# Transfers of 16x16 diagonal blocks through memory, issued by GpSimd in place of ScalarE

## The reference

```python
L = jnp.where(strict, jnp.einsum('nbhcd,nbhsd->nbhcs', k_beta, kb) * decay, 0.0)
eye = jnp.eye(C, dtype=L.dtype)
tinv = lax.linalg.triangular_solve(eye + L, jnp.broadcast_to(eye, L.shape),
                                   left_side=True, lower=True, unit_diagonal=True)
u = jnp.einsum('nbhcs,nbhse->nbhce', tinv, v_beta)
w = jnp.einsum('nbhcs,nbhsd->nbhcd', tinv, k_beta * jnp.exp(gc)[..., None])
```

## Time and profile before

| | us |
|---|---|
| median of 3 runs | 2109.6 (2106.55 to 2113.05) |
| the profiled execution, its own time | 2120.13 |
| its span | 2118.4 |
| TensorE busy | 1952.8 (92%) |
| DVE busy | 1248.9 (59%) |
| ACT busy | 939.3 (44%) |
| GpSimd busy | 4.9 (0%) |

### The profile page before, as it was taken

One profiled execution on the slowest core, in us unless ns is written; L12 is line 12 of the kernel. 1 busy time (PEld: TensorE's weight loads), 2 busy tenths in 40 slices (PEclk: granted clock), 3 DMA queues, 4 the chain that ended last, 5 costly groups with the idle time before them and its releaser, 6 DMA issues.

```text
span 2118.4 us, 45367 instructions
## 1 busy us (share of the span) xinstructions
PE 1952.8 (92%) x19408; PEld 1762.3 (83%) x19408; DVE 1248.9 (59%) x2135; ACT 939.3 (44%) x1834; POOL 4.9 (0%) x30
## 2 busy tenths in 40 slices
PE   6999989899999997899999999988899989879998
PEld 4899968788878876788989998878898778669898
DVE  3455356665445575677556655566654565758863
ACT  3334464344456434333444444544445653343343
POOL 0000000000000000000000000000000000000000
PEclk8999999999999898899999999999899998889999
DMA  7777765556464456698656665544534345267773
GB/s 257 229 228 212 213 172 151 159 145 169 120 177 127 130 150 159 178 265 238 191 158 185 182 176 165 162 123 125 140 103 139 100 117 140 82 138 223 231 199 113
DMA packets 580070, 353.37 MB, mean 167 GB/s; under 512 B 44004, under 2 KB 539654, under 8 KB 578318
## 3 DMA queue, kind: packets, MB, share of 16 engines
q1 hardware_dynamic: 490634, 302.74, 49.7%
q10 hardware_dynamic: 89236, 47.74, 9.1%
HBM read 332.27 MB, written 18.50 MB: 166 GB/s over the span
## 4 chain that ended last, share of the span: by engine, by line
PE 72%; DVE 11%; DMA 7%; ACT 5%; issue 3%; ACTq 3%; SPq 0%; DVEq 0%
PE bank L881 69%; DMA ring<-in_ffn_up 2%; DVE far L1931 2%; DVE ring_r L733 2%; DMA ring<-in_w_ada 2%; ACT w_hi_r L725 1%; DMA far<-in_state_gdn_ssm 1%; DVE big L1931 1%; PE bank L659 1%; ACTq L572 1%; DVE far L1934 1%; PE bank L646 1%; DMA far<-t_blocks 1%; ACTq L627 1%; DVE big L608 1%
## 5 line engine op out<-in xcount | busy, mean ns | idle before, releaser
L881 PE MATMUL bank<-big_r,w_hi_r 128*128 128x264 f32 x4160 | 1082.5, 295 | 37.5 <-DVE h_r L1934 22.7
L881 PE MATMUL bank<-big_r,ring_r 128*128 128x264 f32 (+1 forms) x3456 | 1001.1, 290 | 0.0
L881 PEld LDWEIGHTS bank<-big_r,w_hi_r 128*128 128x128 f32 x4160 | 756.1, 193 | 105.1 <-issue 78.7
L881 PE MATMUL bank<-h_r,w_hi_r 128*128 128x264 f32 x2752 | 804.1, 292 | 0.0
L733 DVE TENSOR_TENSOR ring_r<-ring,w_hi_r 128x1024 fp32r<-128x1024 f32 (+2 forms) x440 | 524.5, 1195 | 466.2 <-ACT w_hi_r L725 462.1
L725 ACT CAST w_hi_r<-ring 128x1024 fp32r<-128x1024 f32 (+2 forms) x440 | 452.3, 1028 | 498.2 <-PE bank L881 262.3
L881 PEld LDWEIGHTS bank<-big_r,ring_r 128*128 128x128 f32 (+1 forms) x3456 | 669.9, 194 | 1.0
L881 PEld LDWEIGHTS bank<-h_r,w_hi_r 128*128 128x128 f32 x2752 | 537.7, 195 | 1.2
L881 PE MATMUL bank<-big,far 64*64 64x64 f32 (+2 forms) x1440 | 106.6, 260 | 0.0
L881 PE MATMUL bank<-ring,c 128*32 128x256 f32 x1152 | 95.4, 413 | 9.4 <-DMA ring<-in_w_ada 6.4
L1931 DVE TENSOR_TENSOR big<-big,bank 128x264 f32<-128x264 f32 (+2 forms) x138 | 62.8, 458 | 56.1 <-PE bank L881 44.2
(11 more groups left out here) (283 smaller groups left out, 1843.7 us busy)
## 6 DMA issues: line engine op xcount, KB each, us to landing
ring<-in_ffn_up SPq DMA_DIRECT2D x176, 512.0 KB, 4.6
ring<-in_w_in SPq DMA_DIRECT2D x148, 512.0 KB, 3.7
ring<-in_w_ada SPq DMA_DIRECT2D x144, 512.0 KB, 4.0
ring<-in_ffn_down SPq DMA_DIRECT2D x64, 512.0 KB, 4.3
far<-in_state_gdn_ssm ACTq DMA_DIRECT2D x28, 512.0 KB, 5.7
ring<-in_ffn_down SPq DMA_DIRECT2D x32, 384.0 KB, 3.5
ring<-in_w_out SPq DMA_DIRECT2D x16, 512.0 KB, 4.7
out_sample_gdn_ssm<-far ACTq DMA_DIRECT2D x16, 512.0 KB, 4.1
```

What stands on the lines that cost most here:

```text
L881: return pe.matmul(out, lhsT, rhs, start=start, stop=stop)
```

## The change

The transfers of the diagonal blocks are issued by GpSimd. Its program for a layer is these 54 transfers and nothing else, in a fixed order, lot by lot, with the waits that ACT had. ACT's program keeps the clearing. The first lot's substitution stands in turns 24 and 25 of DVE's program in place of 20 and 21; the other two lots keep their turns.

```diff
-GATHER0, FETCH0, SOLVE0, STORE0 = (18, 30, 66), (19, 31, 67), (20, 32, 68), (22, 34, 69)
-CLEAR0, SCATTER0, INV0 = (29, 35, 67), (30, 36, 70), (32, 38, 72)
+SOLVE0, CLEAR0, INV0 = (24, 32, 68), (29, 35, 67), (32, 38, 72)
...
-        def gather(act, run):
+        def gather(pool, run):
             lt = inv_sets[run][0]
             if run == 2:
-                act.wait_ge(gdn_dve.sem, gdn_dve.at(H_B - 1))
+                pool.wait_ge(gdn_dve.sem, gdn_dve.at(H_B - 1))
             else:
-                act.wait_ge(prod_dve.sem, prod_dve.at(4 * run + 4))
+                pool.wait_ge(prod_dve.sem, prod_dve.at(4 * run + 4))
...
             for rows, cols, part_of in blocks():
-                act.dma_start(lt_blocks[part_of, :, :].rearrange("u s t -> s u t"), lt[rows, :, cols]).then_inc(block_in.sem, block_in.one())
+                pool.dma_start(lt_blocks[part_of, :, :].rearrange("u s t -> s u t"), lt[rows, :, cols]).then_inc(block_in.sem, block_in.one())
...
             for l in range(DEPTH):
+
+                @block.gpsimd
+                def _(pool):
+                    for run in range(3):
+                        gather(pool, run)
+                        fetch(pool, run)
+                        store(pool, run)
+                        scatter(pool, run)
...
                         for run in range(3):
-                            if t == GATHER0[run] and run < 2:
-                                gather(act, run)
-                            if t == FETCH0[run]:
-                                fetch(act, run)
-                            if t == STORE0[run] and run < 2:
-                                store(act, run)
-                            if t == SCATTER0[run]:
-                                scatter(act, run)
                             if t - INV0[run] == 3:
                                 settled(act, run)
...
-                        if t == GATHER0[2]:
-                            gather(act, 2)
-                        if t == STORE0[2]:
-                            store(act, 2)
...
-                        if t == STORE0[1] + 3:
+                        if t == SOLVE0[1] + 5:
```

More of the change, by code:

```diff
@@ L560, in square, with fetch, store @@
             return buf.rearrange("p (a b) -> p a b", a=B16)
-        def gather(act, run):
+        def gather(pool, run):
             lt = inv_sets[run][0]
             if run == 2:
-                act.wait_ge(gdn_dve.sem, gdn_dve.at(H_B - 1))
+                pool.wait_ge(gdn_dve.sem, gdn_dve.at(H_B - 1))
             else:
-                act.wait_ge(prod_dve.sem, prod_dve.at(4 * run + 4))
+                pool.wait_ge(prod_dve.sem, prod_dve.at(4 * run + 4))
             if run:
-                act.wait_ge(block_in.sem, block_in.at(9 * run))
+                pool.wait_ge(block_in.sem, block_in.at(9 * run))
             for rows, cols, part_of in blocks():
-                act.dma_start(lt_blocks[part_of, :, :].rearrange("u s t -> s u t"), lt[rows, :, cols]).then_inc(block_in.sem, block_in.one())
-        def fetch(act, run):
-            act.wait_ge(block_in.sem, block_in.at(9 * run + 8))
+                pool.dma_start(lt_blocks[part_of, :, :].rearrange("u s t -> s u t"), lt[rows, :, cols]).then_inc(block_in.sem, block_in.one())
+        def fetch(pool, run):
+            pool.wait_ge(block_in.sem, block_in.at(9 * run + 8))
             if run:
[L578 to L583, removed]
+                pool.wait_ge(solved.sem, solved.at(run))
+            pool.dma_start(square(solve_bufs[run][0]), lt_blocks[:, :, :]).then_inc(block_in.sem, block_in.one())
+        def store(pool, run):
+            pool.wait_ge(solved.sem, solved.at(run + 1))
             if run:
-                act.wait_ge(block_out.sem, block_out.at(9 * run))
-            act.dma_start(t_blocks[:, :, :, :], solve_bufs[run][1]).then_inc(block_out.sem, block_out.one())
+                pool.wait_ge(block_out.sem, block_out.at(9 * run))
+            pool.dma_start(t_blocks[:, :, :, :], solve_bufs[run][1]).then_inc(block_out.sem, block_out.one())
         def solve(dve, run, half):
@@ L619, in clear, with scatter @@
             i.then_inc(inv_z.sem, inv_z.one())
-        def scatter(act, run):
-            act.wait_ge(inv_z.sem, inv_z.at(run + 1))
-            act.wait_ge(block_out.sem, block_out.at(9 * run + 1))
+        def scatter(pool, run):
+            pool.wait_ge(inv_z.sem, inv_z.at(run + 1))
+            pool.wait_ge(block_out.sem, block_out.at(9 * run + 1))
             into = inv_sets[run][1].rearrange("p u t w -> p u (t w)")
             for rows, cols, part_of in blocks():
-                act.dma_start(into[rows, :, 2 * cols.start:2 * cols.stop], t_blocks[part_of].rearrange("u s t w -> s u (t w)")).then_inc(block_out.sem, block_out.one())
+                pool.dma_start(into[rows, :, 2 * cols.start:2 * cols.stop], t_blocks[part_of].rearrange("u s t w -> s u (t w)")).then_inc(block_out.sem, block_out.one())
         def invert(pe, run, s):
```

## The result

| | before | with the change |
|---|---|---|
| median, us | 2109.6 (2106.6 to 2113.1, 5 runs) | 2096.6 (2086.3 to 2098.1, 5 runs) |
| ratio, 95% interval | 1 | 0.9926 [0.9899, 0.9952] |
| profiled execution, its own time | 2120.1 | 2086.3 |
| its span | 2118.4 | 2084.6 |

The kernel became faster by 0.7%. The forecast was 2144 us with a range from 2100 to 2205, so it failed, and on the other side. The two profiled executions lie 33.8 us apart and the medians 13: the one of before was longer than all five runs of its median, the one of after was the shortest of its own.

The account below looks back on a forecast made before the run. It took the kernel as bound by TensorE. Transfers' +6.0, +3.6, +3.1 and +4.6 with -0.3 for ACT's freedom and the substitution's move gave 17.0 us a layer, +34 on 2109.6: 2144 us, range 2100 to 2205.

Parts of the forecast that it names:

- d: Time one DMA issue holds GpSimd's queue; taken as 1.25 us, between 0.47 (ACT's median issue) and 3.3 (median landing).
- the four terms of the scatters and the fetch: Later transfers per layer: +6.0 us first scatter, +3.6 lot 1's fetch, +3.1 second scatter, +4.6 lot 2.
- the forecast's own table: Same sums at other d: 0.47 gives 2103 us, 0.7 about nothing, 1.0 2125, 2.0 2208, 3.3 2320.
- what ACT's freedom brings: Issues leaving ACT: -7.5 us a layer, all at turn 18; turns 30, 36 and 70 costed at nothing.
- The new place: First substitution in turns 24 and 25: TensorE's wait 1.29 becomes 6.2 us, clock falls; +8.3 us a layer.
- Turn 18: TensorE's 5.42 us wait behind ACT's issues falls to 1.29; with the clock regained, -7.5 us a layer.
- the old place of the substitution: Turn 21: TensorE's wait of 2.44 us falls to 1.29 once the substitution leaves; -1.1 us a layer.
- The fetch of lot 1: DVE waits about 4 us for the fetch before lot 1's substitution, delaying TensorE's third product: +3.6 us a layer.
- Cheap issues: Rival, chance 0.12: GpSimd issues cost below 0.7 us, so the kernel gets faster, 2103 us.
- DVE shuts GpSimd out: Rival, chance 0.06: GpSimd writes descriptors only while DVE rests, so an issue costs 3.0 us; near 2295 us.
- about 1 us to the first byte: Skill page's figure for GpSimd-issued DMAs, against 0.6 from ACT; as the whole queue hold it would give 2125 us.

Follow-up runs that it names:

- e5: Kernel before with lot 0's transfers alone on GpSimd, lots 1 and 2 on ACT, substitution in turns 20 and 21: 2098.9 us, ratio 0.9945.
- e3: Kernel before with all transfers on GpSimd, first substitution left in turns 20 and 21: 2087.0 us, ratio 0.9888 to the kernel before.
- e8: All transfers on GpSimd, first substitution in turn 23, joining of lots 0 and 1 one turn later: 2109.1 us, ratio 0.9987 to the kernel before.
- e1: The changed kernel run once more, unaltered: 2096.1 us, ratio 0.9927 to the kernel before.
- e2: All transfers on GpSimd, first substitution in turns 23 and 24 instead of the changed kernel's 24 and 25: 2081.7 us, ratio 0.9859 to the kernel before.
- e12: Repeat of the kernel with all transfers on GpSimd and first substitution in turn 23: 2084.2 us, ratio 0.9867 to the kernel before.
- e4: Kernel before, transfers still on ACT, only the first substitution moved to turns 24 and 25 (store at turn 27): 2120.9 us, ratio 1.0033.

## Why the prediction was wrong

**The failed step: the size of d.** "I take their geometric middle, 1.25 us." It is 0.56, near the lower bound, which came from the row for issues; the upper one, the landing, was a row of something else. Nearer still was the earlier trace rows, where ACT's eight issues of a gather took 4.39 us, 0.55 each. A geometric middle between an issue and a landing says nothing about issues. The way of reckoning was right: the same sums with 0.56 give the first scatter's product at 446.9 + 4.5 + 4.6 = 456.0 (measured 455.84), DVE's substitution of lot 1 at 462.2 (463.25), the second scatter's at 484.1 + 4.5 + 4.6 = 493.2 (493.49). So the four terms of the scatters and the fetch, 17.3 us a layer together, fell to about nothing. By interpolation in the forecast's own table d = 0.56 is some -2 us a layer, about 2105; this step alone is 39 of the 47 us by which the forecast missed. (The +3.6 for the fetch is 3.5 by its own figures, 481.1 - 477.6, which changes nothing.)

**The second failed step: what ACT's freedom brings.** "I cost their leaving ACT at nothing" for turns 30, 36 and 70, because TensorE there waits for the transfers. e5 to e3 gives 12 us for lots 1 and 2, 6 a layer. The forecast had the price beside it ("each would give back up to 4 us") and gave it no chance. It read the waits for the transfers rightly, they did not shrink (10.4 before, 10.7 now); but behind lot 2's issues DVE waited for ACT and TensorE's clock fell, and ACT's wait of 4.54 us at the store, which holds a cast of weights, it did not count at all. 12 us is more than the 8 between 2105 and 2096.6; the spread of the runs lets no finer account be made.

**The new place** was right in kind and nearly in size: 1.29 + 4.9 = 6.2 forecast, 5.96 and 6.49 measured, and the clock at 0.58 behind it; 8.3 us a layer forecast, 6.8 and 7.3 by the traces. **Turn 18** too: 5.42 became 1.28, and the clock came back; by ACT's casts it gained 8.9 and 9.0 us a layer together with the old place of the substitution, where 8.6 was forecast; lot 0 alone, with the substitution left at its place (e5), gave 11 us where 15 was forecast.

**The fetch of lot 1.** The wait of DVE of 4 us was there in the first layer, 4.62, and TensorE's third product behind it waits 1.72 us against 0.96; in the second layer DVE waits 0.82. So this was mostly cover, as e8 showed from the other side.

**The rivals.** "Cheap issues", at 0.12, was the truth, and its own number, 2103, is still 6 us too high: it too had no term for lots 1 and 2 on ACT. "DVE shuts GpSimd out" fell: the scatter's issues take 562 ns at the median and 583 at most while DVE works beside them. The Trainium skill's "SBUF — State Buffer", section "Who interferes with whom", names `copy`, `cast` and `tensor_scalar` as the instructions of DVE that can take the ports it shares with GpSimd. The trace does not contradict it and does not test it: beside the scatter of lot 0, from 446.9 to 451.4, DVE ran TENSOR_TENSOR and SCALAR_TENSOR_TENSOR alone. The other page used, "DMA: Bandwidth & Descriptors" with about 1 us to the first byte, does not bear on the hold: GpSimd is free after 0.56 us. Nor does the trace show later landings throughout: a gather lands 3.0 us after its issue where it took 3.3 from ACT, a scatter 3.9 where it took 4.1; but a fetch lands after 3.1 us (2.6 to 2.7 in the traces of e1, e2 and e12) where it took 2.1. Whether that is the first byte is not shown.

Summed up by the experiments: lot 0 -11, lots 1 and 2 -12, the substitution's move +9, together -14 us; measured -13. With the +9 taken from e1 less e3 this sum closes by the way it is made, and is no check; with the move's price from e4, +7 to +11, it is -16 to -12.

## What to carry to other kernels

An unknown price is to be taken from the rows of the same kind of thing, not from a middle to a row of another kind; where the result turns on one such number, the chances should be spread over its whole table and not laid on one point. An engine that issues many small DMAs in its instruction stream pays for it with everything behind them, also where the engine that sets the time is seen waiting for the transfers themselves; and a DMA that must itself wait (here the store, for the substitution) is paid for in the same way. And before a wait is removed, look who else uses it as cover: a wait of 3.6 us taken from TensorE came back as one of 7.0.

## What the runs showed of the hardware

A DMA of 256 short pieces held GpSimd 0.562 us, one of 128 pieces 0.528; on ACT the same DMAs of 256 pieces took 0.31 to 1.55. GpSimd's issues hardly vary: the eight of the gather of lot 1 took 4.44 us in the changed kernel, with the DMA engines' share at 1.11 in those 4.4 us, and the eight of the second scatter 4.47 at a share of 0.47. Two executions of one kernel differed by 15.0 us in TensorE's busy time at the same 19408 instructions, with mean granted clocks of 0.959 and 0.953, which is as much as the change itself is worth.
